# HGRN level-zero products read the even, then the odd columns of the scaled queries; the weights' low part is computed behind the query update

## The reference, cut to what matters

```python
f_fwd = lb[0] + (1.0 - lb[0]) * jax.nn.sigmoid(to_heads(hg_ff, HG_HEADS))
o_fwd = hgrn2_scan(q_h, 1.0 - f_fwd, v_h, jnp.log(f_fwd))
# S_t = diag(f_t) S_{t-1} + k_t v_t^T,   o_t = S_t^T q_t
```

## Time and profile before

| | |
|---|---|
| median of 3 runs | 2547.8 us (2546.92 to 2549.47) |
| the profiled execution's own time | 2547.08 us |
| its span | 2545.3 us |
| PE busy | 2522.3 us, 99% |
| DVE busy | 1638.6 us, 64% |
| ACT busy | 912.7 us, 36% |
| granted TensorE clock | 0.999 of full speed |
| the 8 heads of the HGRN branch | about 562 to 1120 us of the span |

### The profile page before, as it was taken

How to read it: one execution, slowest core, us unless ns; L and a number is a source line. 1 busy time by engine, 2 the same in 40 slices (tenths; PEclk the granted TensorE clock), 3 DMA queues, 4 the chain that set the end, 5 groups by cost and what they waited for, 6 DMA issues and landing times.

```text
span 2545.3 us, 33468 instructions
## 1 busy us (share of the span) xinstructions
PE 2522.3 (99%) x13110; PEld 2151.8 (85%) x13110; DVE 1638.6 (64%) x1864; ACT 912.7 (36%) x1122; POOL 749.0 (29%) x713
## 2 busy tenths in 40 slices
PE   9999999999999999999999999999999999999998
PEld 9888888889999999988887888876788888888887
DVE  6675555248888888866655424433457898887567
ACT  6342222133334333432333433333333443343433
POOL 2032232002221121234442001167413456553001
PEclk9999999999999999999999999999999999999999
DMA  8323333432223323344444536155514233225755
GB/s 296 120 95 109 100 124 108 141 134 98 85 100 108 108 99 109 108 158 144 155 149 161 186 124 215 34 183 204 175 45 146 91 109 133 100 100 198 273 191 182
DMA packets 181628, 349.67 MB, mean 137 GB/s; under 512 B 10459, under 2 KB 106023, under 8 KB 181472
## 3 DMA queue, kind: packets, MB, share of 16 engines
q1 hardware_dynamic: 119520, 154.44, 18.1%
q0 software_dynamic: 33088, 118.51, 13.3%
q10 hardware_dynamic: 28864, 74.59, 8.0%
HBM read 241.16 MB, written 106.33 MB: 137 GB/s over the span
## 4 chain that ended last, share of the span: by engine, by line
PE 95%; DMA 2%; DVE 1%; ACT 1%; issue 0%; POOL 0%; SPq 0%; ACTq 0%; DVEq 0%; POOLq 0%
PE ps L2302 17%; PE ps L2852 13%; PE ps L2441 12%; PE ps L2870 8%; PE ps L2333 7%; PE ps L2682 6%; PE ps L2508 4%; PE ps L2820 3%; PE ps L2465 3%; PE ps L2591 3%; PE ps L2612 2%; PE ps L2630 2%; PE ps L2380 2%; PE ps L2535 2%; PE ps L2793 1%; PE ps L2618 1%
## 5 line engine op out<-in xcount | busy, mean ns | idle before, releaser
L2302 PE MATMUL ps<-a_hi,whi 128*128 128x512 f32 x576 | 234.2, 407 | 0.0
L2302 PE MATMUL ps<-a_hi,wlo 128*128 128x512 f32 x576 | 224.8, 390 | 0.0
L2302 PE MATMUL ps<-a_lo,whi 128*128 128x512 f32 x576 | 224.4, 390 | 0.0
L1621 DVE TENSOR_TENSOR wlo<-raw,whi 128x2048 fp32r<-128x2048 f32 x59 | 135.9, 2304 | 112.0 <-ACT whi L997 110.9
L997 ACT ACTIVATE whi<-raw 128x2048 fp32r<-128x2048 f32 x59 | 113.1, 1917 | 192.4 <-PE ps L2682 105.1
L1002 ACT ACTIVATE ev<-ps 128x512 f32<-128x512 f32 x128 | 76.5, 598 | 209.7 <-PE ps L2302 131.7
L2333 PE MATMUL ps<-whi,a_hi 128*128 128x256 f32 x512 | 148.0, 289 | 0.0
L2333 PE MATMUL ps<-whi,a_lo 128*128 128x256 f32 x512 | 144.8, 283 | 0.0
L2333 PE MATMUL ps<-wlo,a_hi 128*128 128x256 f32 x512 | 144.8, 283 | 0.0
L793 POOL TENSOR_TENSOR cv<-cv,cs 128x1024 f32<-128x1024 f32 x16 | 38.5, 2406 | 321.3 <-ACT cs L1261 321.3
L2302 PEld LDWEIGHTS ps<-a_hi,wlo 128*128 128x128 f32 x576 | 108.1, 188 | 23.5
(11 more groups left out here) (422 smaller groups left out, 7188.1 us busy)
## 6 DMA issues: line engine op xcount, KB each, us to landing
raw<-in_w_in SPq DMA_DIRECT2D x45, 1024.0 KB, 6.4
raw<-in_w_up SPq DMA_DIRECT2D x22, 1024.0 KB, 5.0
hg_T<-ev ACTq DMA_DIRECT2D x32, 512.0 KB, 3.0
qfb<-hg_T POOLq DMA_DIRECT2D x24, 512.0 KB, 5.4
wd<-in_w_down POOLq DMA_DIRECT2D x44, 256.0 KB, 3.6
down_weight_sums<-wd POOLq DMA_DIRECT2D x22, 512.0 KB, 4.4
hidden_T<-ga ACTq DMA_DIRECT2D x11, 1024.0 KB, 4.0
hidden_sums<-s POOLq DMA_DIRECT2D x10, 1024.0 KB, 4.9
```

Source lines behind the costliest of these rows:

```text
L1621: signal(dve, dve.tensor_tensor(wlo[:, b.slot], w4[:, b.slot], whi[:, b.slot], ALU.subtract), w_lo, b.count())
L2302: ins = pe.matmul(ps[:, unit_bank(b, u)], W[sw][:, b.slot, k, c * P:(c + 1) * P], op[mw][:, k, t * HALF:(t + 1) * HALF], start=k == 0 and ...
```

## The change

It does three things at level 0 of every head; the other six levels are as before. (1) The moving view of `X` takes the 64 even columns of the first half, then the 64 odd columns of the second half; before, it alternated between them. (2) The scores now lie in PSUM in that order, so the predicated copy puts them back: it reads PSUM in two runs of 64 and writes `Am`, and reads the mask, with a step of 2. (3) `split_lo(bN)` stands behind the query update of level 0 in place of before it, and so ahead of the predicated copy.

```diff
                     signal(dve, dve.tensor_tensor(view(Y, 0, *dims), view(Y, 0, *dims),
                                                   view(a, o + nb_ + 1, [-nb_ - 1, 2], [2, nb_ // 2], [0, hh]), ALU.mult),
                            h_updy, h * LEVELS + l + 1)
-                    if l == 0:
-                        split_lo(bN)
                     dve.wait_ge(h_lv, h * 8 + l + 2)
                     dve.tensor_tensor(view(X, 0, *dims), view(X, 0, *dims),
                                       view(a, o + 1, [nb_ - 1, 2], [2, nb_ // 2], [0, hh]), ALU.mult).then_inc(h_upd, 1)
+                    if l == 0:
+                        split_lo(bN)
...
-                    signal(dve, dve.copy_predicated(Am[:], lmask[:, l:l + 1].to_broadcast([P, NT, P]),
-                                                    psw[:, b0:b0 + D].rearrange("p (c t) -> p c t", c=NT)),
-                           h_pred, h * LEVELS + l + 1)
+                    if l == 0:
+                        ins = dve.copy_predicated(view(Am, 0, [P, NT], [1, 2], [2, P // 2]),
+                                                  view(lmask, 0, [0, NT], [1, 2], [2, P // 2]),
+                                                  view(psw, b0, [P, NT], [P // 2, 2], [1, P // 2]))
+                    else:
+                        ins = dve.copy_predicated(Am[:], lmask[:, l:l + 1].to_broadcast([P, NT, P]),
+                                                  psw[:, b0:b0 + D].rearrange("p (c t) -> p c t", c=NT))
+                    signal(dve, ins, h_pred, h * LEVELS + l + 1)
...
-                    dims = ([2 * hh, P // (2 * hh)], [T + hh, 2], [1, hh])
+                    dims = ([2 * hh, P // (2 * hh)], [T + hh, 2], [1, hh]) if l else ([T + 1, 2], [2, P // 2])
```

## The result

Over 22 runs of each kernel the median went from 2546.71 us to 2552.03 us; the ratio is 1.0020, with a 95% interval of 1.0014 to 1.0026. By that ratio the change made the kernel slower by 5.1 us (3.6 to 6.6), against a forecast of 2.4 us less. One of the 22 runs of the changed kernel took 6487.15 us at a granted clock of 1.0, for no reason that the record shows; it is in the median and not in the ratio. The profiled execution has a span of 2549.5 us, against 2545.3.

The account below looks back on a forecast made before the run. TensorE (PE) bounds the kernel, busy for 99% of the span. Faster reads at level 0 (-6.2 us), a wait at level 2 (+3.8) and the copy at +0 make -2.4: 2547.8 to 2545.4 us, range 2541.0 to 2548.5, expected "same".

Parts of the forecast that it names:

- the price of the predicated copy: DVE, level 0: the copy with stepped Am and mask was to stay at 1307 ns, +0.
- Nearest row: DVE, level 0: query update with a step of 2 in place, 1227 ns against 1226, taken as basis for +0.
- The other bound: ACT's key copy takes 1.55 against 1.06 when alternating halves; by that factor the predicated copy would be 0.6 us longer.
- The case itself: Rival: stepped predicated copy at level 0 is slow; if doubled, 10.4 us added, 2555.8 us; chance 0.09, 0.04 in milder size.
- the range: Whole kernel: 2541.0 to 2548.5 us, widened down for the no-wait case and up by 1.5 us for a longer wait.
- the signs of being wrong: Profile: copy above 1.5 us, level 2's load on time, level 0's pace above 5, any wait at level 1, 5 or 6.
- the prediction's own sum: Over 8 heads: -6.2 us from level 0's reads plus 3.8 us of PE's wait at level 2, -2.4 us.
- The pace of level 0: PE, load of level 0 to load of level 1: from 5.41 to 4.64 us, 0.77 us a head, 6.2 us in all.
- The wait at level 2: PE waits for the DVE's query update of level 1: E + 7.48 against E + 7.01, 0.47 us a head, 3.8 us.
- Level 1, 5 and 6: PE's loads: no wait; level 1's update ends E + 1.33, load due E + 2.37; level 6 keeps 0.45 us room.
- the low part and the next weight block: `half_N` reads the low part 30 us later; SP's next block goes out some 2.7 us later; cost nothing.
- The rival of no wait: Before level 2 PE doesn't wait, so the gain stands whole: -6.2 to -7.0, 2540.8 to 2541.6 us; chance 0.14.

Follow-up runs that it names:

- the sixth kernel: Low part in its old place; the DVE's write to Am at level 0 differs by head: plain copy and in-place update stepped by 2 1.22 us, predicated 2.46.
- the head with the 3.96 us wait: Changed kernel with all three operands of level 0's predicated copy alternating between columns 64 apart in this head: copy 4.78 us, level 2's pace 5.76.
- the first experiment: Changed kernel with another form of level 0's predicated copy in each head: 2.46 us where Am is stepped, 4.78 all alternating, about 1.3 otherwise.
- the last test of the copy: Low part in its old place; level 0's writes to Am in runs, pairs or steps by head; head 8, predicated copy stepped by 8, took 4.57 us.

## Why the prediction was wrong

**The step that failed is the price of the predicated copy.** It was set at +0, by what the prediction called the "Nearest row": the query update with a step of 2, 1227 ns against 1226. That row tells the truth for its own kind, an update without a predicate, and the multiplication in place of the sixth kernel shows the same for Am (1.22 us). It doesn't carry over to a predicated write (2.46). The other bound, a factor from ACT's key copy, gave 0.6 us and was too low as well; the measured 1.15 lay outside both. The case itself stood among the rivals, with the right place and rule ("Each 0.1 us here is 0.1 us more of PE's wait", measured 1.15 for 1.15), the point from which it decides (0.94 us) and 0.09 as its chance. That chance was too small for an operation of which no row had this form, and the range, which ended at 2548.5, left it out. A copy above 1.5 us was named among the signs of being wrong, and it is the one that came. With 1.15 us on each copy the prediction's own sum gives -2.4 + 9.2 = +6.8; the measured 5.1 is less, mainly by two small terms on the other side, 0.08 us a head more gain at level 0 and 0.11 us a head that come back behind the wait.

Point by point:
- **The pace of level 0**: taken as 4.64, measured 4.56, so the gain is 0.85 in place of 0.77 a head, 6.8 in place of 6.2. A step of 2 in one half is a shade better than pairs that alternate between halves. By the Trainium skill's sentence on lines of 16 bytes in "SBUF — State Buffer", section "Specifications (TRN2)", it would have been 4.54; the trace agrees to 0.02 us.
- **The wait at level 2**: 0.47 forecast, 0.48 where it was measured with a copy of 1.31 us, 1.63 in the changed kernel. Its mechanism held in all kernels that had it. Not counted was that 0.11 us come back at the next level (4.43 in place of 4.54). PE isn't faster there. The load starts 0.22 us ahead of its product at level 3 (648.60 and 648.82) but together with it behind the wait (644.17 and 644.18), so the load's lead, lost at the wait, is won back:
```profile
644.18 2.05 PE L2513 MATMUL ps<-X,Yc 128*128 128x128 f32 x16 [1.21 <-DVE X L1861]
648.82 1.95 PE L2513 MATMUL ps<-X,Yc 128*128 128x128 f32 x16
```
- **Level 1, 5 and 6** have no waits, and the low part and the next weight block are late for nobody: as forecast.
- **The sum with the measured terms**: 8 x (-0.85 + 0.48 + 1.15 - 0.11) = +5.4, by the rounded terms, against 5.1 measured. With the copy at +0 it is -3.8, and the kernel with the copy of before measured -3.8; with an interval of -6.1 to -1.5 that they agree to the tenth is luck.
- **The range**: its upper end was added up wrongly. The smallest gain with the longest wait is 2547.8 - 6.2 + 4.6 = 2546.2, not 2547.0, and 1.5 us more makes 2547.7, not 2548.5. The measured time lies above both.
- **The rival of no wait** is wrong for this change, but right for its view: with the low part back, -6.1 and -5.6 us were measured.

## What to carry to other kernels

Take the price of a strided operand from a row of the same operation, with the same operand strided: a step that is free for a plain write nearly doubled the predicated copy, and the reordering could be had for nothing on its read side. If no row has the form, give its worst size a real chance when it lands on the chain. A wait can cost more than its own length, as the head with the 3.96 us wait showed. And before work is moved "behind" an urgent instruction, add up the chain to the next urgent one of the same engine: cover beside the products (2.3 us here) was given up for a level that was not late, and paid at the one after it.

## What the runs showed of the hardware

- A predicated copy on the DVE (float32 output, byte mask) goes by visits to 16-byte groups of its output: about 0.16 us + 1.15 us for 256 visits, a fit to these copies. 1024 columns: 1.31 in order, 2.46 with a step of 2 (2.45 in pairs 4 apart), 4.77 with a step of 4, 4.57 with a step of 8, 4.78 with all three operands alternating 64 apart. A start that is off by two columns nearly doubles runs of 4 (0.70 to 1.29).
- The byte mask may have a step of 2, and a source in PSUM a step of 2 or columns that alternate 64 apart, at no cost (1.31 or 1.32). A source in SBUF was only read in order (1.32), and no mask with a larger step was tried by itself.
- Plain float32 writes of the DVE: 1.22 us in order and with a step of 2, 1.96 alternating 64 apart, 1.99 and 2.05 with steps of 4 and 8.
- PE's moving operand in float32: a step of 2 costs 0.02 us over running columns (4.56 against 4.54), over 8 products of 128 columns +0.39 us when it alternates 64 columns apart, +0.87 between halves, +1.7 to +1.9 with steps of 4 to 16.
- The granted TensorE clock: after PE had stood idle for 3.54 us (head 5 of the first experiment) it was 0.50 in the next 1.9 us and 1.00 again from 861.50 us on. After 1.92 us of idle time (head 4 of the kernel on writes) it was 0.58 in the stretch from 783.00 to 785.20, and the 16 products took 3.62 us. After 1.71 us (head 8 of the last test of the copy) it stayed at 1.00, and they took 2.05.
